# Transposing x unscaled as it arrives, with the norm weight as a factor per partition, in a two-block mixer kernel

## The reference, cut to what matters

```python
def rms_norm(x, w):
    xf = x.astype(jnp.float32)
    y = xf * lax.rsqrt(jnp.mean(xf * xf, axis=-1, keepdims=True) + NORM_EPS)
    return (y * w.astype(jnp.float32)).astype(x.dtype)
...
        h = rms_norm(x, pre_norm_w[l])
        y = hybrid_mixer(h, w_in[l], ...)      # proj = h @ w_in
```

## Time and profile before

| | us |
|---|---|
| median of 3 runs | 1326.43 |
| lowest, highest run | 1325.88, 1328.53 |
| span of the profiled execution, first to last instruction | 1324.9 |
| TensorE busy in that span | 1280.8 (97%) |
| VectorE busy | 797.9 (60%) |
| ScalarE busy | 614.3 (46%) |
| DMA | 224.58 MB, mean 170 GB/s |

### The profile page before, as it was taken

One profiled execution on the slowest core, in us unless ns is written; L12 is line 12 of the kernel. 1 busy time (PEld: TensorE's weight loads), 2 busy tenths in 40 slices (PEclk: granted clock), 3 DMA queues, 4 the chain that ended last, 5 costly groups with the idle time before them and its releaser, 6 DMA issues. The chain is left out here.

```text
span 1324.9 us, 17917 instructions
## 1 busy us (share of the span) xinstructions
PE 1280.8 (97%) x7296; PEld 1110.6 (84%) x7296; DVE 797.9 (60%) x1064; ACT 614.3 (46%) x869; POOL 22.8 (2%) x36
## 2 busy tenths in 40 slices
PE   7999999999999999999999999799999999999996
PEld 6999988998998878888888888678888787878885
DVE  5668776764775455546454555567466766466553
ACT  4555545223422445543444444254445555466443
POOL 0100000000000000000000000000000000000000
PEclk9999999999999999999999999899999999999998
DMA  8646554444444454566666686455645654454662
GB/s 276 181 128 193 177 184 131 128 128 134 127 138 130 128 176 140 174 189 191 189 193 187 193 318 197 128 190 162 188 143 159 192 159 143 143 192 155 223 193 79
DMA packets 119778, 224.58 MB, mean 170 GB/s; under 512 B 9409, under 2 KB 20833, under 8 KB 118545
## 3 DMA queue, kind: packets, MB, share of 16 engines
q1 hardware_dynamic: 118386, 213.81, 52.9%
q0 software_dynamic: 1312, 9.63, 2.0%
HBM read 219.22 MB, written 4.19 MB: 169 GB/s over the span
## 5 line engine op out<-in xcount | busy, mean ns | idle before, releaser
L1076 DVE TENSOR_TENSOR lo_w<-raw_w,hi_w 128x1024 fp32r<-128x1024 f32 x396 | 479.5, 1221 | 337.2 <-ACT hi_w L740 336.3
L740 ACT ACTIVATE hi_w<-raw_w 128x1024 fp32r<-128x1024 f32 x396 | 410.2, 1055 | 287.5 <-PE acc L1645 202.7
L1645 PE MATMUL acc<-hi_w,h_hi 128*128 128x512 f32 (+1 forms) x832 | 333.3, 401 | 2.9 <-DVE h_lo L1084 2.6
L1645 PE MATMUL acc<-hi_w,h_lo 128*128 128x512 f32 (+1 forms) x832 | 322.8, 388 | 0.0
L1645 PE MATMUL acc<-lo_w,h_hi 128*128 128x512 f32 (+1 forms) x832 | 321.9, 387 | 0.0
L1645 PEld LDWEIGHTS acc<-hi_w,h_hi 128*128 128x128 f32 x832 | 157.5, 189 | 34.3 <-issue 5.0
L1636 PE MATMUL acc<-h_hi,hi_w 128*128 128x256 f32 x640 | 184.4, 288 | 1.4 <-DVE lo_w L1076 1.4
L1645 PEld LDWEIGHTS acc<-hi_w,h_lo 128*128 128x128 f32 x832 | 157.0, 189 | 33.1
L1645 PEld LDWEIGHTS acc<-lo_w,h_hi 128*128 128x128 f32 x832 | 157.6, 189 | 29.7 <-issue 0.7
L1636 PE MATMUL acc<-h_hi,lo_w 128*128 128x256 f32 x640 | 181.0, 283 | 0.0
L1636 PE MATMUL acc<-h_lo,hi_w 128*128 128x256 f32 x640 | 180.9, 283 | 0.0
(11 more groups left out here) (319 smaller groups left out, 1262.0 us busy)
## 6 DMA issues: line engine op xcount, KB each, us to landing
raw_w<-in_w_in SPq DMA_DIRECT2D x284, 512.0 KB, 3.8
raw_w<-in_w_out SPq DMA_DIRECT2D x64, 512.0 KB, 4.7
raw_w<-in_w_branch_a SPq DMA_DIRECT2D x16, 512.0 KB, 4.5
raw_w<-in_w_branch_b SPq DMA_DIRECT2D x16, 512.0 KB, 4.7
raw_w<-in_cmp_k_w SPq DMA_DIRECT2D x8, 512.0 KB, 4.3
raw_w<-in_cmp_v_w SPq DMA_DIRECT2D x8, 512.0 KB, 4.1
x_in<-in_x SPq DMA_DIRECT2D x4, 512.0 KB, 6.0
x<-in_x POOLq DMA_DIRECT2D x1, 2048.0 KB, 10.5
```

The lines of the kernel that those rows point to most:

```text
L740: act.activation(hi_w[slot][:, 0:n], raw_w[no % RAW_SLOTS][:, 0:n], ACT.Copy).then_inc(*hi_ready.event(no))
L1076: dve.tensor_tensor(lo_w[slot][:, 0:n], raw_w[no % RAW_SLOTS][:, 0:n], hi_w[slot][:, 0:n].bitcast(F32), ALU.subtract).then_inc(*lo_ready.e ...
L1645: i = pe.matmul(to[:, t, 0:group.cols], x[at], w[:, k], start=first and k == 0 and m == 0, stop=last and k == n - 1 and m == 2)
```

## The change

What it does, part by part:

- x is loaded in eight transfers of 256 KB (one quarter of the columns of one token tile each), issued by ScalarE instead of SP, quarter 0 first. SP's queue starts with the norm weight and `ident`, then comes straight to weight piece 0.
- The norm weight is loaded as 16 rows of 128 values, transposed once by TensorE into a 128 x 16 tile, and copied to `norm_col`. The four spreading matmuls are gone.
- TensorE transposes x itself (`x_in`). VectorE then multiplies the transposed tile in `aux` by `norm_col`, one factor per partition and k tile, into `xs` in SBUF. ScalarE makes `h_hi` from `xs`, VectorE `h_lo` from `xs`. A bank of `aux` is free again after the multiplication.
- `scale_x` is gone as a step; quarter 2 is transposed and scaled at tick 1 instead of 0, quarter 3 at tick 3 instead of 1. Ahead of the list, pieces 0 and 1 are both split between quarter 0 and quarter 1.
- The products no longer wait for the accumulator banks to be released by `scale_x`.
- Of `r1_row`, the building of the diagonal stays at tick 6 as a step `r1_diag`; TensorE's matmul and VectorE's copy move to tick 7.

```diff
     for n in (2, 3):
-        at(n - 2, "scale_x", n)
         for t in range(NT):
-            at(n - 2, "flip", "h1", n, t)
+            at(2 * n - 3, "flip", "h1", n, t)
...
-    at(6, "r1_row")
+    at(6, "r1_diag")
+    at(7, "r1_row")
...
         @block.sync
...
-            sp.dma_start(ident[:], ins["ident"]).then_inc(*row_ready.event(0))
-            sp.dma_start(row1[:], ins["pre_norm_w"]).then_inc(*row_ready.event(1))
-            for m in range(2):
-                for t in range(NT):
-                    cols = slice(m * D // 2, (m + 1) * D // 2)
-                    sp.dma_start(x_in[:, t, cols], x[:, t, cols]).then_inc(*x_ready[2 * m + t].event(0))
+            sp.dma_start(norm_rows[:], ins["pre_norm_w"][0].rearrange("(k p) -> k p", p=P)).then_inc(
+                *row_ready.event(0))
+            sp.dma_start(ident[:], ins["ident"]).then_inc(*row_ready.event(1))
...
         @block.scalar
+            x = ins["x"][0].rearrange("(t p) d -> p t d", p=P)
+            for n in range(4):
+                for t in range(NT):
+                    cols = slice(n * COLS, (n + 1) * COLS)
+                    act.dma_start(x_in[:, t, cols], x[:, t, cols]).then_inc(*x_ready[n][t].event(0))
...
             def flip(name, n, t):
+                if name == "h1":
+                    act.wait_ge(*dve_did.after("x_scaled", n, t))
+                    source = xs[:, t, quad(n)]
...
-            for n in range(2):
-                for t in range(NT):
-                    flip("h1", n, t)
-                split(n)
+            for t in range(NT):
+                flip("h1", 0, t)
+            split(0)
+            split(1)
+            for t in range(NT):
+                flip("h1", 1, t)
...
         @block.vector
+            def scaled(name, n):
+                for t in range(NT):
+                    dve.wait_ge(*flip_filled.after(name, n, t))
+                    dve.tensor_tensor(xs[:, t, quad(n)], aux[:, flip_bank(name, n, t)].rearrange("p (k c) -> p k c", k=QUAD),
+                                      over_cols(norm_col[:, quad(n)]), ALU.mult).then_inc(*dve_did.event("x_scaled", n, t))
+                for t in range(NT):
+                    lower(name, n, t, xs[:, t, quad(n)])
...
-            dve.wait_ge(*pe_did.after("row1"))
-            scale_x(0)
-            scale_x(1)
-            for n in range(2):
-                for t in range(NT):
-                    flip("h1", n, t)
-                split(n)
+            dve.wait_ge(*pe_did.after("norm_col"))
+            link(dve.tensor_copy(norm_col, aux[:, 3, 0:KT]))
+            scaled("h1", 0)
+            split(0)
+            split(1)
+            scaled("h1", 1)
...
         @block.tensor
-                elif first:
-
-                    pe.wait_ge(*flip_source.after("h1", 2 * g_ + 1, 1))
...
-            pe.wait_ge(*pool_did.after("ones"))
-            for n in range(4):
-                last = pe.matmul(acc[:, n // 2, n % 2], ones[0:1, :], row1[:, n * COLS:(n + 1) * COLS], start=True,
-                                 stop=True)
-            last.then_inc(*pe_did.event("row1"))
+            take(3, (dve_did, "x_scaled", 0, 0))
+            turn(aux[:, 3, 0:KT], norm_rows[:]).then_inc(*pe_did.event("norm_col"))
```

More of the change, by code:

```diff
@@ L377, in build @@
         gnorm_w = place("gnorm_w", [P, P], F32)
-        small = place("small", [P, 400], F32)
+        small = place("small", [P, 416], F32)
         half = place("half", [P, 16], F32)
@@ L386, in bit @@
             top[0] += n
-            assert top[0] <= 400
+            assert top[0] <= 416
             return small[:, top[0] - n:top[0]]
         dt_row, alog_row, sink_row = bit(HEADS), bit(HEADS), bit(16)
+        norm_col = bit(KT)
         r1, ry, r2, r3 = bit(NT), bit(NT), bit(NT), bit(NT)
@@ L430, in build @@
         x_in = arena("x_in", [P, NT, D], F32, 48)
-        row1 = arena("row1", [1, D], F32, 64)
-        xw = arena("xw", [P, NT, D], F32, 72)
+        norm_rows = arena("norm_rows", [KT, P], F32, 64)
+        xs = arena("xs", [P, NT, KT, P], F32, 72)
         mzs = arena("mzs", [P, NT, HEADS, P], F32, 56)
@@ L488, in build @@
         raw_ready = [signal(f"raw_ready{i}", 16) for i in range(RAW_SLOTS)]
-        x_ready = [signal(f"x_ready{i}", 16) for i in range(2 * NT)]
+        x_ready = [[signal(f"x_ready{n}{t}", 16) for t in range(NT)] for n in range(4)]
         row_ready = signal("row_ready", 16)
@@ L587, in _ @@
         def _(sp):
-            x = ins["x"][0].rearrange("(t p) d -> p t d", p=P)
-            sp.dma_start(ident[:], ins["ident"]).then_inc(*row_ready.event(0))
-            sp.dma_start(row1[:], ins["pre_norm_w"]).then_inc(*row_ready.event(1))
-            for m in range(2):
-                for t in range(NT):
-                    cols = slice(m * D // 2, (m + 1) * D // 2)
-                    sp.dma_start(x_in[:, t, cols], x[:, t, cols]).then_inc(*x_ready[2 * m + t].event(0))
+            sp.dma_start(norm_rows[:], ins["pre_norm_w"][0].rearrange("(k p) -> k p", p=P)).then_inc(
+                *row_ready.event(0))
+            sp.dma_start(ident[:], ins["ident"]).then_inc(*row_ready.event(1))
             def load(no):
@@ L758, in flip @@
             def flip(name, n, t):
-                b = flip_bank(name, n, t)
-                act.wait_ge(*flip_filled.after(name, n, t))
+                source = aux[:, flip_bank(name, n, t)].rearrange("p (k c) -> p k c", k=QUAD)
+                if name == "h1":
+                    act.wait_ge(*dve_did.after("x_scaled", n, t))
+                    source = xs[:, t, quad(n)]
+                else:
+                    act.wait_ge(*flip_filled.after(name, n, t))
                 hi = LHS[name][0]
-                act.activation(hi[:, quad(n), t * P:(t + 1) * P],
-                               aux[:, b].rearrange("p (k c) -> p k c", k=QUAD), ACT.Copy).then_inc(
+                act.activation(hi[:, quad(n), t * P:(t + 1) * P], source, ACT.Copy).then_inc(
                     *flip_hi.event(name, n, t))
@@ L767, in sq1 @@
                 t = n % 2
+                for c in range(n // 2 * 2, n // 2 * 2 + 2):
+                    act.wait_ge(*x_ready[c][t].after(0))
                 squares([(x_in[:, t, c * COLS:(c + 1) * COLS], sum1[:, t * 4 + c:t * 4 + c + 1])
@@ L1079, in flip, with lower @@
             def flip(name, n, t):
-                b = flip_bank(name, n, t)
+                if name == "h1":
+                    if t == 0:
+                        scaled(name, n)
+                    return
+                lower(name, n, t, aux[:, flip_bank(name, n, t)].rearrange("p (k c) -> p k c", k=QUAD))
+            def lower(name, n, t, source):
                 dve.wait_ge(*flip_hi.after(name, n, t))
@@ L1083, in flip @@
                 at = (slice(None), quad(n), slice(t * P, (t + 1) * P))
-                dve.tensor_tensor(lo[at], aux[:, b].rearrange("p (k c) -> p k c", k=QUAD), hi[at].bitcast(F32),
-                                  ALU.subtract).then_inc(*flip_lo.event(name, n, t))
+                dve.tensor_tensor(lo[at], source, hi[at].bitcast(F32), ALU.subtract).then_inc(
+                    *flip_lo.event(name, n, t))
+            def scaled(name, n):
[5 more added lines that the diff above has]
+                    lower(name, n, t, xs[:, t, quad(n)])
             def ba_():
@@ L1119, in beta_gcum @@
                 dve.tensor_tensor(beg, beta, eg, ALU.mult).then_inc(*dve_did.event("beg"))
-            def scale_x(n):
-                cols = slice(n * COLS, (n + 1) * COLS)
-                for t in range(NT):
-                    dve.wait_ge(*x_ready[n // 2 * 2 + t].after(0))
-                    dve.tensor_tensor(xw[:, t, cols], x_in[:, t, cols], acc[:, n // 2, n % 2], ALU.mult).then_inc(
-                        *flip_source.event("h1", n, t))
             def norm1():
@@ L1142, in ba_split, with r1_diag_ @@
                 dve.wait_ge(*block2_rows.after(8))
-            def r1_row_():
+            def r1_diag_():
                 dve.wait_ge(*pool_did.after("r1"))
@@ L1149, in r1_row_ @@
                 last.then_inc(*dve_did.event("r1_diag"))
+            def r1_row_():
                 dve.wait_ge(*pe_did.after("r1_row"))
@@ L1161, in raw_out @@
                     dve.wait_ge(*act_did.after("sq1", 3))
-                    dve.wait_ge(*flip_source.after("h1", 3, 1))
+                    dve.wait_ge(*flip_filled.after("h1", 3, 1))
                 dve.tensor_tensor(raw[:], channels_of(END[("conv", part, h)]), over_heads(r1_row[:]), ALU.mult).then_inc(
@@ L1528, in finish @@
                     dve.tensor_scalar(y, y, r3[:, 1:2], None, ALU.mult).then_inc(*dve_did.event("finish", m))
-            dve.wait_ge(*pe_did.after("row1"))
-            scale_x(0)
-            scale_x(1)
-            for n in range(2):
-                for t in range(NT):
-                    flip("h1", n, t)
-                split(n)
-            steps = {"scale_x": scale_x, "norm1": norm1, "small_rows": small_rows, "ba_split": ba_split,
```

(15 more changed lines are left out.)

## The result

The changed kernel took 1333.09 us (median of 5, 1330.14 to 1334.86) against 1326.44 (also 5 runs); the ratio is 1.0043, with a 95% interval from 1.003 to 1.0055. That is 5.7 us more, outside the range and on the other side of the forecast. The one slower rival had named the clock in the front as its cause, and that is not what happened. The profiled execution took 1331.37 with a span of 1329.4, 4.5 above the span of before.

A forecast was written before the change was run, and what follows sets the result against it. TensorE, busy 97% of 1324.9 us, bounds the kernel, and piece 5's landing limits the front's gain. 2.1 gained at tick 8 minus 1.0 for the clock is 1.1: 1326.4 - 1.1 = 1325.3, range 1321.9 to 1328.4.

The forecast's parts named there:

- slower rival: Ahead of ticks 5 and 6: TensorE's clock falls in the pauses and stays down, 3.8 us lost, 1330.2; chance 0.11.
- the signs that I had named for being wrong: Piece 5 by 27 or ScalarE not idle (faster); clock 0.50 over 8 us in first 60 (slower); new pause elsewhere (queues misread).
- First products: Front of TensorE: the first products start at 10.0 us against 15.79 before, bounds 10 and 14.
- Piece 5: SP's queue: this weight piece lands at 28.4 us, 0.8 earlier than before; ScalarE idles 3 to 4 us for it.
- Landing to tick 6: From piece 5's landing through its split, quarter 3, squares and piece 6's split: 8.0 us, tick 6 starting at 36.4.
- L: The time at which piece 5's transfer lands, taken as 28.4 us against 29.2 before.
- The clock: TensorE's granted clock drops to 0.50 after a pause in the front, as once for 3.41 us; 1.0 us taken as lost.
- the second pause: TensorE's pause ahead of tick 6, 2.8 us; nothing is lost if the clock drop falls into the other pause.
- Diagonal: The 1.13 us wait at the diagonal of `r1` is gone, as it is built a tick earlier.
- The mark: Start of tick 8's products: 42.8 us against 44.9 before, 2.1 gained, ahead of 1.0 for the clock.
- The rival with L at 26.4: Piece 5 lands up to 2.8 us earlier through two queues: 3.3 to 4.1 gained, 1322.3 to 1323.1; chance 0.20.
- The 3.5 us and the 2 us for a low clock in ticks 0 and 1: Low clock in the front: ticks 0 and 1 cost up to 3.5 us, hidden; up to 2 with piece 5 in time.

The follow-up runs named there:

- the fastest run: Changed kernel with `small` at 400 columns, `norm_col` in a free arena corner, pieces 5 to 8 issued ahead of the large constants: 1321.49 us, ratio 0.9944.

## Why the prediction was wrong

- *The step that failed* is in the first paragraph: "A change that touches only the first 45 us can therefore give no more than what TensorE idles or does slowly there, and a gain survives to the end." The change also touches where 1152 later matmuls find their operand. I costed every instruction and every DMA, and did not cost the 16 columns added to `small`; the full diff has them, the excerpt ahead of the prediction leaves them out. The missing term is +7.6 us (1152 matmuls at 233.3 instead of 226.8 ns), and the run with the kernel before and nothing but the 16 columns shows it alone: 1.0048. The slower rival looked in the front too, and none of the signs that I had named for being wrong showed: the low clock there lasted 6.82 us, under the 8, and there was no new pause elsewhere.
- *First products:* forecast 10.0, measured 11.08. The term that was short is the arrival of quarter 0: I took 5.2, and its second transfer landed at 6.14, the 6.1 that I had worked out for the weights taking half. `ident`, which I had let hide, landed at 5.11 and held TensorE's first transpose until 5.15. With `ident` earlier the second set of four transposes could have begun only 0.1 sooner, at 6.14 instead of 6.27.
- *Piece 5:* forecast 28.4, landed 28.8. The wait on ScalarE was forecast at 3 to 4 us and was 4.48. Right in mechanism and size.
- *Landing to tick 6:* forecast L + 8.0, measured 36.87 - 28.75 = 8.1. Right, and 8.1 again in the four other traces where piece 5 binds, with L from 27.7 to 32.5.
- *The clock:* the pause ahead of tick 5 was followed by 6.82 us at the low level, which is longer than the 3.41 that I priced. It fell into the second pause, as I had allowed for, which shrank from 2.8 to 0.18.
- *Diagonal:* no wait ahead of it, as forecast.
- *The mark:* forecast 42.8 and 1.0 for the clock, that is 43.8; measured 43.58. The closeness is in part luck: L came 0.35 later and tick 6 another 0.1, and the clock cost 0.3 instead of 1.0. The forecast gain of 1.1 was 1.3 behind the mark. Without the shift of the arena the timed gain was 3 to 5 us, above my size.
- *The rival with L at 26.4* needed two queues to fill the slow start. They did not go beyond 382 GB/s. I had moved L by the earlier issue of x alone, as if queues and order made no other difference. In the run with x on SP's queue, ahead of the weights, piece 5 lands 3.7 later, so they do make one. That 28.4 came close to 28.8 does not show that my reason for it was right.
- *Numbers that do not follow:* without any clock loss the sum gives 1326.4 - 2.1 = 1324.3, not the 1323.8 at the lower end of my range. The 3.5 us and the 2 us for a low clock in ticks 0 and 1 came from no row. In the fastest run, where piece 5 was early, these ticks took 1.7 us longer than at full speed.

## What to carry to other kernels

Read a diff for what it does to addresses, not only to instructions: a tile that grows moves all that is placed behind it, and in this kernel 64 bytes made each 512-column fp32r matmul 2 to 3% longer wherever the two operands no longer started alike modulo 256 bytes. Comparing the same instruction's start in both traces, late in the program, finds such a loss at once, because it grows without any pause. And an input made early is worth only what the next input behind it allows: moving piece 5 ahead of the constants in the queue gave 2.4 us in one comparison and 2.5 in the other, beside 3 to 5 for the whole restructured front.

## What the runs showed of the hardware that I had not expected

- The pace of the fp32r matmuls of 512 columns depends on the starts of the stationary and the moving operand relative to each other: 226.7 ns from start to start (228 with h) when they agree modulo 256 bytes (shifts of 0, 256 and 512, or all moved together), 232.4 to 233.4 ns at 32, 64 and 128 bytes off. The loss is the same where no other engine and no transfer is at work (233.4 against 226.7 ns).
- In the products of 256 columns with the roles exchanged, a shift of 64 bytes between the operands went the other way: 117.8 for 119.8 ns.
- Between 5 and 10 us, one queue with x in 256 KB transfers ahead of the weights moved 252 GB/s, where two queues side by side moved 382. The number of queues and the order changed together.
